# Five edits to a one-core transformer block: where the last expert rows are added, a half step, and the first 30 microseconds

## The reference

```python
# block 1: sliding-window attention with a sink per head (4 heads, 128-token blocks)
m = max(max(logits), sink)
p = exp(logits - m)
probs = p / (sum(p) + exp(sink - m))
# block 1: cross attention to 256 memory rows
mkv = rms_norm(mem, mem_norm_g) @ w_mem_kv
# block 2, last stage: routed experts (32 experts, 2 per token, hidden width 256)
h = rmsnorm(x, ffn_norm)
out = sum over the 2 experts e of a token:  share_e * ((silu(h @ w_gate[e]) * (h @ w_up[e])) @ w_down[e])
x = x + out
```

## Time and profile before

| | |
|---|---|
| median of three executions | 1346.6 us |
| profiled execution | 1345.78 us |
| its span (first to last record) | 1343.9 us |
| granted TensorE clock, mean | 0.988 of full speed |
| PE busy | 1277.1 us, 95% |
| DVE / ACT / POOL busy | 596.9 / 382.1 / 695.7 us |
| SP's first transfer issued | 0.74 us |
| bytes moved by POOL's DMA queue (gathers, scatters, overflow weights) | 8.44 MB |

### The profile page before, as it was taken

The page is one execution under the profiler, slowest core; times in us unless marked ns, Lnnn a source line. Parts: engine busy times, 40 slices in busy tenths (PEclk is TensorE's granted clock), DMA queues, the critical chain, the costliest instruction groups (busy, mean ns, idle before and its releaser), DMA issues.

```text
span 1343.9 us, 19020 instructions
## 1 busy us (share of the span) xinstructions
PE 1277.1 (95%) x7493; PEld 920.8 (69%) x7493; DVE 596.9 (44%) x984; ACT 382.1 (28%) x757; POOL 695.7 (52%) x719
## 2 busy tenths in 40 slices
PE   6999989999999999999999999999998999999992
PEld 5888768787787767888888877788786333333330
DVE  2252361448982683627765788624226011111013
ACT  4311262422333683112224533611121111111110
POOL 6666636576675302766872655775930433333320
PEclk9999999999999999999999999999999999999996
DMA  6533211432132201242222124732383899999945
GB/s 224 161 103 100 94 32 22 157 117 94 64 127 94 95 2 32 94 157 84 74 79 79 57 59 154 284 109 93 113 357 109 318 383 380 384 379 390 388 199 198
DMA packets 85454, 216.39 MB, mean 161 GB/s; under 512 B 23717, under 2 KB 32629, under 8 KB 71797
## 3 DMA queue, kind: packets, MB, share of 16 engines
q1 hardware_dynamic: 62124, 199.22, 40.1%
q0 software_dynamic: 13824, 8.44, 2.1%
q10 hardware_dynamic: 9416, 7.51, 1.7%
HBM read 255.99 MB, written 26.22 MB: 210 GB/s over the span
## 4 chain that ended last, share of the span: by engine, by line
PE 82%; DVE 5%; POOL 4%; ACT 2%; issue 2%; DMA 2%; DVEq 1%; POOLq 1%; SPq 0%; ACTq 0%
PE ps L141 17%; PE ps L143 17%; PE ps L142 17%; PE ps L1108 12%; PE ps L1120 6%; POOL w_lo L1156 3%; PE ps L1100 2%; PE ps L793 2%; POOL w_hi L1153 2%; PE ps L914 1%; PE ps L998 1%; DMA xg<-rows_scratch,row_u 1%; POOLq L1154 1%; DMA back<-y_scratch 1%; PE ps L922 1%
## 5 line engine op out<-in xcount | busy, mean ns | idle before, releaser
L1156 POOL TENSOR_TENSOR w_lo<-stage,w_hi 128x512 fp32r<-128x512 f32 (+1 forms) x296 | 391.4, 1353 | 11.1 <-issue 0.7
L1153 POOL CAST w_hi<-stage 128x512 fp32r<-128x512 f32 (+1 forms) x296 | 193.4, 695 | 378.8 <-PE ps L143 349.6
L141 PE MATMUL ps<-hi,w_hi 128*128 128x512 f32 (+1 forms) x608 | 237.0, 390 | 0.6 <-ACTq L1492 0.5
L142 PE MATMUL ps<-hi,w_lo 128*128 128x512 f32 (+1 forms) x608 | 235.0, 387 | 0.0
L143 PE MATMUL ps<-lo,w_hi 128*128 128x512 f32 (+1 forms) x608 | 235.0, 386 | 0.0
L141 PE MATMUL ps<-w_hi,hi 128*128 128x512 f32 (+1 forms) x488 | 176.2, 361 | 4.9 <-POOL w_lo L1156 4.3
L142 PE MATMUL ps<-w_hi,lo 128*128 128x512 f32 (+1 forms) x488 | 174.7, 358 | 0.0
L143 PE MATMUL ps<-w_lo,hi 128*128 128x512 f32 (+1 forms) x488 | 174.7, 358 | 0.0
L1108 PE MATMUL ps<-w_gu,xT 128*64 128x512 f32 x768 | 170.1, 595 | 0.4 <-DVE xT L2312 0.4
L141 PEld LDWEIGHTS ps<-hi,w_hi 128*128 128x128 f32 x608 | 114.2, 188 | 27.5 <-issue 3.0
L2312 DVE TENSOR_TENSOR xT<-ps,ffn_kp 128x1024 f32<-128x1024 f32 x24 | 29.4, 1225 | 232.9 <-PE ps L1108 215.5
(11 more groups left out here) (451 smaller groups left out, 1679.3 us busy)
## 6 DMA issues: line engine op xcount, KB each, us to landing
stage<-w_in SPq DMA_DIRECT2D x84, 512.0 KB, 4.5
w_gu<-w_gate SPq DMA_DIRECT2D x32, 1024.0 KB, 10.6
w_gu<-w_up SPq DMA_DIRECT2D x32, 1024.0 KB, 12.9
w_dn<-w_down SPq DMA_DIRECT2D x32, 1024.0 KB, 12.8
stage<-w_out SPq DMA_DIRECT2D x16, 512.0 KB, 4.6
stage<-w_ssd_branch SPq DMA_DIRECT2D x16, 512.0 KB, 4.8
stage<-w_in SPq DMA_DIRECT2D x20, 256.0 KB, 3.0
stage<-w_attn_branch SPq DMA_DIRECT2D x8, 512.0 KB, 4.2
```

Of the source, the lines that this page charges most:

```text
L141: pe.matmul(out, x[0], w[0], start=first, stop=False)
L142: pe.matmul(out, x[1], w[0], start=False, stop=False)
L1153: nc.gpsimd.tensor_copy(hi[:, b, k, 0:n], stage[:, b, k, 0:n])
L1156: last = nc.gpsimd.tensor_tensor(lo[:, b, k, 0:n], stage[:, b, k, 0:n], hi[:, b, k, 0:n].bitcast(F32), ALU.subtract)
```

## The change

**Start.** SP loads `memb` before the parameter rows, and no longer waits for the parameters. ACT takes one root of a constant before it waits for `memb`; behind it the program has one table load in place of two. PE runs 20 transposes of the identity while it waits. `unit_m` is made by two `tensor_scalar` instructions. The first half tile is split by two engines: POOL casts piece by piece, DVE subtracts piece by piece; POOL starts the second half tile when DVE is done.

**Sink.** The sink is the start value of the maximum and is copied as a 257th column behind the scores, so that the exponentials' sum has it. L1810, L1812, L1295 and L1775 go; one copy of 128x4 comes in.

**Half step.** The overflow pairs are turned by one: step 2 takes the last pair, which can have one slot only, steps 5 to 23 take pairs 0 to 6. Step 2 is a half step: its hidden units are divided over the two halves of the array's columns. Steps 22 and 23 are now pair 15 and overflow pair 6. `turn_slot(2)` moves behind `down(0)`, `turn_slot(3)` moves before `down(1)`.

**Last two steps.** Their rows are not scattered. Zeros are scattered to their rows early. ACT and DVE scale the results by each row's share and split them into `yh` and `yl`; PE multiplies them by a matrix of zeros and ones (`place_r`), which puts each row at its token, and DVE adds the sums to `xres`. The shares are written to memory by eight transfers of 128 elements of 4 bytes and gathered by two indirect transfers. The load of `back` starts behind the scatter of step 21. The output goes out in eight half tiles.

**Semaphores.** The gates' saves share one semaphore `z_saved`.

```diff
-            for dst, src in params[1::2]:
+            sp.dma_start(memb[:], d["mem"][0].rearrange("(t p) n -> p t n", p=P)).then_inc(mem_in, 16)
+            for dst, src in params[1::2]:
                 sp.dma_start(dst, src).then_inc(par_in, 16)
-            sp.dma_start(memb[:], d["mem"][0].rearrange("(t p) n -> p t n", p=P)).then_inc(mem_in, 16)
-            sp.wait_ge(par_in, PARAMS)
...
+                if i == 5:
+                    sp.wait_ge(rt_step, 4)
+                    for k in range(2):
+                        for t in range(TT):
+                            sp.dma_start(share_dram[S * k + P * t:S * k + P * (t + 1), :], share[:, k, t:t + 1]).then_inc(share_saved, 16)
...
-            for b in range(3):
-                sp.wait_ge(y_out[b], 16 * (STEPS // 3))
+            sp.wait_ge(slots_set, 32)
+            for s in range(LAST[0] - 3, LAST[0]):
+                sp.wait_ge(y_out[s % 3], 16 * (s // 3 + 1))
+            sp.wait_ge(dn_done, LAST[0])
...
+            idle(ps[s][:, 3, 0:P], 20)
             pe.wait_ge(mem_in, 16)
...
+            def project_half():
+                pe.wait_ge(gu_in[4], 32)
+                for k in range(KC):
+                    for f in range(2):
+                        last = pe.matmul(p_gu[halves[f]][:, 0:HID], xT[:, k, halves[0]], w_gu[4][:, :, k, f:HID:2],
+                                         start=(k == 0), stop=(k == KC - 1))
+            def down_half():
...
+                for c in range(2):
+                    for f in range(2):
+                        last = pe.matmul(p_dn[halves[0], c, :], actT[:, 0, halves[f]], w_dn[4][:, f, 512 * c:512 * (c + 1)], start=(f == 0), stop=(f == 1))
...
+            def place(j, c, t):
+                for y in (yh[j], yl[j]):
+                    last = pe.matmul(p_out(c, t), place_r[j][:, t, :], y[:, c, :], start=(j == 0 and y is yh[0]), stop=(j == 1 and y is yl[1]))
+                if j == 1:
+                    last.then_inc(out_full, 1)
...
-                if s < 2:
+                if s in (0, 2):
                     turn_slot(s + 1)
...
                     down(s - 1)
-                    if s + 2 < STEPS:
+                    if s == 1:
+                        turn_slot(2)
+                    elif s + 2 < STEPS:
                         turn_slot(s + 2)
...
+            pool.wait_ge(w_in_sem[0], 32)
+            for k in range(HALF):
+                nc.gpsimd.tensor_copy(w_hi[:, 0, k], stage[:, 0, k]).then_inc(first_hi, 1)
+            pool.wait_ge(w_in_sem[1], 32)
+            pool.wait_ge(w_split, 1)
+            split(1, 512)
...
+            def high(s):
+                j = LAST.index(s)
+                A.wait_ge(slots_set, 64)
+                A.wait_ge(y_out[s % 3], 16 * (s // 3))
+                for c in range(2):
+                    A.wait_ge(dn_done, LAST[0] + 2 * j + c + 1)
+                    A.activation(yh[j][:, c], ps[1][:, c, :], ACT.Copy, scale=slot_share[:, j:j + 1]).then_inc(y_ready, 1)
...
+            for k in range(HALF):
+                V.wait_ge(first_hi, k + 1)
+                last = V.tensor_tensor(w_lo[:, 0, k], stage[:, 0, k], w_hi[:, 0, k].bitcast(F32), ALU.subtract)
+            last.then_inc(w_split, 1)
...
+            V.wait_ge(slots_set, 64)
+            V.wait_ge(dn_done, LAST[0])
+            for c in range(2):
+                low(0, c)
+            for t in range(2):
+                add_back(t)
+            for c in range(2):
+                low(1, c)
+            add_back(2)
+            for c, t in ((0, 0), (0, 1), (0, 2)):
+                add_placed(c, t)
+            add_back(3)
+            for c, t in ((0, 3), (1, 0), (1, 1), (1, 2), (1, 3)):
+                add_placed(c, t)
```

More of the change, by code:

```diff
@@ L356, in program @@
         out_ready = sem("out_ready")
+        share_saved, slots_set, placing, out_full = sem("share_saved"), sem("slots_set"), sem("placing"), sem("out_full")
         out_done = sem("out_done")
@@ L1139, in _ @@
                     down(s - 1)
-                    if s + 2 < STEPS:
+                    if s == 1:
+                        turn_slot(2)
+                    elif s + 2 < STEPS:
                         turn_slot(s + 2)
                 pe.wait_ge(act_ready, s + 1)
-                for f in range(2):
-                    last = pe.transpose(p_act[:, P * f:P * (f + 1)], act[:, f:HID:2], ident[:])
+                if s == HALF_STEP:
+                    last = pe.transpose(p_act[:, 0:P], act[:, 0:P], ident[:])
+                else:
+                    for f in range(2):
+                        last = pe.transpose(p_act[:, P * f:P * (f + 1)], act[:, f:HID:2], ident[:])
                 last.then_inc(act_turned, 1)
             down(STEPS - 1)
+            pe.wait_ge(placing, 3)
+            for c, t in OUT_ORDER[0:6]:
+                place(0, c, t)
+            pe.wait_ge(placing, 4)
+            for c, t in OUT_ORDER[0:4]:
+                place(1, c, t)
+            pe.wait_ge(placing, 5)
+            for c, t in OUT_ORDER[4:6]:
+                place(1, c, t)
+            for c, t in OUT_ORDER[6:8]:
+                for j in range(2):
+                    place(j, c, t)
         @block.gpsimd
@@ L2359, in _ @@
                     V.wait_ge(act_turned, s)
-                V.tensor_tensor(act[:], sa[:], ps[0][:, 0, HID:2 * HID], ALU.mult).then_inc(act_ready, 1)
+                n = HID // 2 if s == HALF_STEP else HID
+                V.tensor_tensor(act[:, 0:n], sa[:, 0:n], ps[0][:, 0, n:2 * n], ALU.mult).then_inc(act_ready, 1)
+                if s == LAST[0]:
+                    for j in range(2):
+                        row = slot_row[:, j, :]
+                        last = V.tensor_tensor(place_r[j][:], bc(iota[:], 1, TT), bc(row, 2, P), ALU.is_equal)
+                    last.then_inc(placing, 1)
+                if s == 3:
+                    for j in range(2):
+                        q = pair_of(LAST[j])
+                        V.tensor_copy(slot_row[:, 2, j:j + 1], row_u[:, q:q + 1])
+                        V.drain()
+                        V.tensor_scalar(slot_row[:, j, :], token[:, 0:TT], token[:, 0:1], slot_row[:, 2, j:j + 1], ALU.subtract, ALU.subtract)
+                        V.drain()
+                        V.tensor_scalar(slot_row[:, j, :], slot_row[:, j, :], -1.0, None, ALU.mult)
+                        V.drain()
                 if s == 0:
```

192 lines of the change are left out of this document (119 added, 73 removed).

## The result

Four executions took 1333.23 to 1336.41 us, median **1334.8**; the kernel before, beside it on the same chip, 1345.96. The ratio is 0.9914, 95% interval 0.9893 to 0.9935: faster by 11 us, half of the 20.9 forecast, and 1.8 us outside the range. The profiled execution took 1333.23 us (span 1331.4, clock 0.994), 12.55 less than that of before.

The account below looks back on a forecast made before the run. PE, busy 95% of the span, was taken to bound the kernel. Gains of 4.5 + 3.3 + 5.85 + 7.2 = 20.85 us took 1345.78 to 1324.9, and 0.8 for the median made 1325.7; range 1319 to 1333.

Parts of the forecast that it names:

- Start, 4.5: Start of the kernel: the split of the second half tile on POOL ends at 21.4 for 26.0; 4.5 us counted, bounds 3.6 to 5.6.
- rival 1: Start and sink: DVE and POOL take turns at a shared port; start gives 3.6, sink 0.7, time 1329.2; chance 0.18.
- so its chain moves along: Start: `x` is asked for sooner and its sums stood behind the memory rows on ACT, so its work moves too; no separate size.
- Sink, 3.3: Attention: 1.7 of PE's 2.85 us wait go and 1.6 come back from the clock; 3.3 us, bounds 0.7 to 4.5.
- the clock's, 1.6: Attention, behind PE's wait: about 3.3 us ran at half rate; the clock should now hold, giving back 1.6 us.
- Expert stage, 5.85: From the end of `project(1)` to the start of `project(3)`: 21.75 us become 15.9, a gain of 5.85.
- At no cost: writes of the shares: Expert stage: eight share writes, 3.6 us of SP ahead of a weight request, covered by the weights' lead of 35 us.
- 0 to 4 us: Expert stage: cost to PE of each item called free, such as the share writes, if its cover were missing.
- End, 7.2: After the last steps: DVE is the bound and the span ends at 1336.5; gain 7.4, 7.2 counted, bounds 4 to 8.
- Rival 2: Expert stage: the clock falls at the new 1.7 us gap before step 2, 1.7 us lost, time 1327.4; chance 0.10.
- Rival 4: End: loads back and outputs collide, or PSUM additions wait for PE; the end gives 3, time 1330; chance 0.07.
- Rival 5: Expert stage: gathered rows arrive late behind weights, 4.1 us a step; with seven such steps 1354.4, slower; chance 0.02.

Follow-up runs that it names:

- first_params: Kernel after, with three parameter loads asked for first and PE's two products waiting for these alone, not all 29: 1334.25 us, ratio to before 0.9908.
- before_with_writes: Kernel before, with only the eight writes of the shares in pieces of 4 bytes added, read by nobody: 1354.66 us, ratio 1.0053.
- combined_old_sink: Kernel after with shares as 8 rows of 512 bytes by one issue, three parameter loads ahead, 12 idle PE turns, but the old sink: 1327.8 us.
- one_issue_small: Kernel after, with the 1024 shares still in pieces of 4 bytes but sent by one issue on SP in place of eight: 1340.25 us, ratio 0.9953.
- early_pieces: Kernel after, with its eight writes of 4-byte pieces asked for before the first refill of weights, not before the fourth: 1342.34 us, ratio 0.9963.

## Why the prediction was wrong

**Start, 4.5: right in its place, wrong behind it.** The split took 4.41 us (9.46 to 13.87), between the 3.0 of full overlap and the 5.0 of taking turns: a cast and a subtraction each took some 0.25 longer beside the other (0.82 for 0.57, 0.91 for 0.69). Turns taken in full, the rule of rival 1, would have been the 5.0; the measurement is between. The step that failed stands behind that: "so its chain moves along" follows the chain to `x`, which held, and the 4.5 was then carried to the end of the kernel with nothing set down for the next meeting with a transfer. ACT's 29 parameter loads started 4.42 us sooner, but their issues ended only 1.9 sooner (51.61 to 49.73), because one took 3.5; PE came 4.4 sooner. Cost 2.95 us in this trace, and with the three loads ahead all of the start arrives (4.75).

The mechanism is shown by first_params; its size is not a constant, and part of the 2.95 can be luck. From the `xn` turn to the first `pT` the five traces that have the new start and wait for all 29 loads take 134.88 to 139.41 us, the ten with the three loads ahead 133.13 to 133.21. In the five the last issue ended within 0.4 us of the same time, so what varied is when it landed and what the clock did behind the wait. Nor is the wait only the change's: before_with_writes has the old start, waits 3.09 and takes 139.39, for 133.54 in the trace before. Why the one issue (of `v_g`) takes 2.0 to 3.6 us in every trace of the new start and 0.60 in both of the old one stays open.

**Sink, 3.3: mis-sized, 2.05.** The chain of waits was right. The term that was mis-sized is the clock's, 1.6: the stretch takes 29.53 us with the fall (before) and 29.19 without (combined_old_sink), so half rate in a stretch where DVE and ACT set the pace cost 0.3. That is the whole 1.25. The wait's own 1.7 came as forecast, though the maximum with a scalar start value, which I had priced as unchanged, takes 0.4 of the 2.1 that the new sink gives with a constant.

**Expert stage, 5.85: the step that failed is "At no cost: writes of the shares".** Their cover was said to be 35 us; weights for `project(7)` were asked for at 1092.6 before and wanted at 1116.6, 24 us, of which their own transfer takes 11 to 13 (timeline of the kernel before):

```profile
1092.63 0.43 SPq L498 DMA_DIRECT2D w_gu<-w_gate  x1
...
1116.55 7.09 PE L1108 MATMUL ps<-w_gu,xT 128*64 128x512 f32 x32
```

And 1024 pieces of 4 bytes were priced as "about 4.6 or less" from 512 pieces of 128 bytes landed on idle queues. They took 7.4 to 12.1 to land and 4.91 us of SP, and then DMA moved 105 to 162 GB/s in place of 400. The 4.9 us that they cost are above even the "0 to 4 us" set down for the case without cover. The measure that matters is not when pieces land but the engine time they take, an estimated 0.11 us each, in queues that are busy 0.96 of the time. The Trainium skill (DMA: Bandwidth & Descriptors, "Rules for kernel authors") says to merge many small transfers, and its "Specifications" ask for 512 bytes at least; eight rows of 512 bytes made no dip, so the trace agrees as to the size. Merging the issues and keeping the pieces (one_issue_small) did not help: it is the pieces that have to be merged. It was the rule that spoke against this change, and I weighed two others.

The rest of the stage came out: 5.2 once the pieces are gone, of which 3.4 is the half step and the rest a shorter wait and no fall of the clock behind it. How large that rest is depends on the trace: the old order took 28.75 us from `project(1)` to `project(3)` in before and 27.82 in before_with_writes. The half `down` saves nothing (3.60 and 3.60), so the two halves of the array do run at once, as the Trainium skill (TensorEngine Tiling (Array Packing), "Key Properties") says. Moving the turn was worth nothing that can be told, in the kernels where it was tried (all with the parameters ahead): it trades a wait for a gap of the same size.

**End, 7.2: right, 8.03.** DVE is the bound as forecast: its additions start 11.96 us behind `project(23)`, forecast 11.9. The 0.8 more are small parts: DVE's work took 17.05 us for 17.5 (the additions from PSUM 0.62 each for 0.69), the tail 2.8 for 3.0, and the sum itself gave 7.4, of which 7.2 were counted.

**Rivals.** Rival 1 holds in part: the negation is stretched (1.10), and casts and subtractions took turns in part. Rival 2's place was wrong: the clock held over the gap of 1.71 in all six traces that have it unfilled. It fell behind other waits. Rival 4 did not come. Rival 5 named the right resource with the wrong victim: not the gathers but the weights (in early_pieces it was the gather). The range failed since "0 to 4 us" for the writes was written down but not laid beside a second miss: 4.9 and 2.95, with the sink's 1.25, are 9.1 of the forecast's 20.85. The stage fell short by another 0.65 and the start by 0.1; the end gave 0.8 more than counted and the stretch ahead of the experts 0.65, so 8.35 in all are missing.

## What to carry to other kernels

Before a step is called free because its data are small, count its pieces and ask what is queued behind them: engine time per piece times pieces is the price, and it is paid by whoever shares the queues. When a start is made faster, follow it to every later meeting with a transfer that did not move as far. A wait taken away from PE is worth its length only where PE sets the pace. And before a difference of one or two us between two traces is put down to an edit, look for a fall of the clock or a late landing that one of them has in a place that the edit doesn't touch.

## What was not expected of the hardware

- A piece of 4 bytes costs about 0.11 us of one DMA engine (an estimate, from the windows of the kernel after), and behind one transfer of 1024 pieces the next two issues on its queue took 3.42 and 1.53 us, where such an issue takes 0.4 to 0.7 in one_issue_large.
- Waits of equal length differ in what the clock does behind them. Behind 1.65 and 1.66 us (for `q_col`) it held in one_issue_small and fell in the kernel after; it held behind 2.86 us in combined_old_sink and fell behind 2.85 in the kernel before. Behind one and the same wait of 2.1 us near 850 it fell in 9 traces and held in 8.
- A per-row start value makes the 128x256 add-and-maximum 0.48 us for 0.42, and the next one starts 0.41 behind it for 0.35.
- POOL's scaling of 128x1024 takes 2.84 to 3.23 us, more than its addition of two such tiles (2.34), and was followed once by 7.76 us of nothing.
